# A two-layer transformer trunk on one core: the seven non-final experts of the first round written as straight code on TensorE, VectorE, ScalarE and SyncE

## What is computed

```python
def moe_swiglu(h, w_router, w_gu, w_down):
    t = h.reshape(-1, D)                                # 256 x 1024
    logits = (t @ w_router).astype(jnp.float32)
    top_val, top_idx = lax.top_k(logits, TOP_K)         # 2 of 8
    top_w = jax.nn.softmax(top_val, axis=-1)
    gates = jnp.sum(jax.nn.one_hot(top_idx, N_EXPERTS) * top_w[..., None], axis=1)
    out = jnp.zeros_like(t)
    for e in range(N_EXPERTS):
        out = out + gates[:, e:e + 1] * swiglu(t, w_gu[e], w_down[e])
    return out.reshape(B, S, D)
```

## Time and profile before

| | us |
|---|---|
| median of 3 runs | 1356.4 (1354.75 to 1358.1) |
| the profiled execution's own time | 1348.95 |
| its span, first to last instruction | 1347.1 |
| its mean granted TensorE clock | 0.979 of full |

### The profile page before, as it was taken

One profiled execution on the slowest core, in us unless ns is written; L12 is line 12 of the kernel. 1 busy time (PEld: TensorE's weight loads), 2 busy tenths in 40 slices (PEclk: granted clock), 3 DMA queues, 4 the chain that ended last, 5 costly groups with the idle time before them and its releaser, 6 DMA issues.

```text
span 1347.1 us, 41800 instructions
## 1 busy us (share of the span) xinstructions
PE 1289.3 (96%) x18773; PEld 859.4 (64%) x18773; DVE 416.9 (31%) x658; ACT 237.0 (18%) x377; POOL 78.1 (6%) x101
## 2 busy tenths in 40 slices
PE   6999999999999999999899899989989998999996
PEld 4499999899776666665566455545645564566653
DVE  6867778788851001101010110010110011002003
ACT  3254443465730001001000000000000000000001
POOL 2610000000120000000000000000000000000001
PEclk9999999999989999999899899989989998999998
DMA  9998999779199999999999999989999999999980
GB/s 360 409 344 296 331 320 338 280 273 383 50 388 408 408 390 397 408 402 404 343 409 398 344 392 398 409 300 406 398 343 388 398 410 326 393 395 396 410 323 34
DMA packets 210338, 478.39 MB, mean 355 GB/s; under 512 B 15072, under 2 KB 38704, under 8 KB 210032
## 3 DMA queue, kind: packets, MB, share of 16 engines
q1 hardware_dynamic: 204928, 457.76, 89.2%
q0 software_dynamic: 5088, 17.59, 4.3%
q10 hardware_dynamic: 144, 0.26, 0.1%
HBM read 465.98 MB, written 11.15 MB: 354 GB/s over the span
## 4 chain that ended last, share of the span: by engine, by line
PE 94%; issue 3%; DVE 1%; ACT 1%; DMA 1%; POOL 0%; SPq 0%; DVEq 0%; POOLq 0%
PE ps L2152 44%; PE ps L2159 22%; PE ps L1698 7%; PE ps L1700 7%; PE ps L1699 7%; PE ps L1789 1%; DMA raw<-w_mod 1%; PE ps L1778 1%; PE ps L1682 1%; PE ps L1986 0%; PE ps L2117 0%; PE ps L1716 0%; PE ps L2075 0%; PE ps L2108 0%; PE ps L1756 0%
## 5 line engine op out<-in xcount | busy, mean ns | idle before, releaser
L2152 PE MATMUL ps<-raw,turned_in 128*32 128x256 f32 x4704 | 276.6, 389 | 28.0 <-issue 28.0
L2152 PE MATMUL ps<-ring_w,turned_in 128*32 128x256 f32 x4560 | 259.3, 379 | 0.0
L2152 PEld LDWEIGHTS ps<-raw,turned_in 128*32 128x32 f32 x4704 | 154.8, 112 | 143.4 <-issue 45.0
L1572 DVE TENSOR_TENSOR tmp<-tmp,ps 128x384 f32<-128x384 f32 x56 | 31.0, 554 | 691.5 <-ACT tmp L1052 691.5
L2152 PEld LDWEIGHTS ps<-ring_w,turned_in 128*32 128x32 f32 x4560 | 147.6, 110 | 101.6
L1052 ACT ACTIVATE tmp<-ps 128x384 f32<-128x384 f32 x56 | 27.4, 490 | 838.9 <-PE ps L2152 838.9
L1698 PE MATMUL ps<-thi,whi 128*128 128x256 f32 x480 | 135.9, 283 | 2.1 <-DVE tlo L1126 2.1
L2159 PE MATMUL ps<-ring_w,turned_act 128*32 128x256 f32 x2352 | 137.6, 380 | 0.0
L1699 PE MATMUL ps<-tlo,whi 128*128 128x256 f32 x480 | 135.8, 283 | 0.0
L1700 PE MATMUL ps<-thi,wlo 128*128 128x256 f32 x480 | 135.8, 283 | 0.0
L2159 PE MATMUL ps<-raw,turned_act 128*32 128x256 f32 x2208 | 125.4, 379 | 0.0
(11 more groups left out here) (281 smaller groups left out, 1014.3 us busy)
## 6 DMA issues: line engine op xcount, KB each, us to landing
raw<-moe_w_gu SPq DMA_DIRECT2D x196, 512.0 KB, 7.0
ring_w<-moe_w_gu SPq DMA_DIRECT2D x190, 512.0 KB, 7.3
ring_w<-moe_w_down SPq DMA_DIRECT2D x98, 512.0 KB, 7.3
raw<-moe_w_down SPq DMA_DIRECT2D x92, 512.0 KB, 7.5
raw<-w_mod SPq DMA_DIRECT2D x88, 512.0 KB, 6.0
rows<-moe_w_gu SPq DMA_DIRECT2D x62, 512.0 KB, 7.7
raw<-ffn_w_gu SPq DMA_DIRECT2D x44, 512.0 KB, 5.5
rows<-moe_w_down SPq DMA_DIRECT2D x34, 512.0 KB, 6.5
```

What stands on the lines that cost most here:

```text
L1572: dve.tensor_tensor(actf_e.rearrange("p (g j) -> p g j", g=GROUPS), sg_e.rearrange("p (g j) -> p g j", g=GROUPS), gate_up_ps(c, 1), ALU.mu ...
L2152: mm = pe.matmul(tile_out(j, 2 * (c % 2) + g // 2, (g % 2) * 256, 256), g_t[:, k, 32 * g:32 * g + 32], w[:, kk, :, :, 32 * j:32 * j + 32], ...
```

## The change

In the first round (`ps_no == 0`) the hardware loops over experts become Python loops, so that each pass is written out, with the expert's number a constant. In the later rounds, behind the `If`, the hardware loops stay. GpSimd is not touched. Nothing in a pass is removed, added or reordered but what handled the expert's number and the loop.

```diff
@@ sync, experts
                 gate_up(0, 0, 0, 0, False, False)
-                with sp.Fori(0, NE - 1) as e:
-                    expert(e, False)
+                if ps_no == 0:
+                    for e in range(0, NE - 1):
+                        expert(e, False)
+                else:
+                    with sp.Fori(0, NE - 1) as e:
+                        expert(e, False)
@@ scalar, experts
                 expert(0, True, False)
-                with act.Fori(1, NE - 1) as e:
-                    expert(e, False, False)
+                if ps_no == 0:
+                    for e in range(1, NE - 1):
+                        expert(e, False, False)
+                else:
+                    with act.Fori(1, NE - 1) as e:
+                        expert(e, False, False)
@@ vector, experts
-                with dve.Fori(1, NE - 1) as e:
-                    expert(e, False, False)
+                if ps_no == 0:
+                    for e in range(1, NE - 1):
+                        expert(e, False, False)
+                else:
+                    with dve.Fori(1, NE - 1) as e:
+                        expert(e, False, False)
@@ tensor, experts
-                with pe.Fori(1, NE - 1) as e:
-                    expert(e, False, False)
+                if ps_no == 0:
+                    for e in range(1, NE - 1):
+                        expert(e, False, False)
+                else:
+                    with pe.Fori(1, NE - 1) as e:
+                        expert(e, False, False)
```

## The result

| | before | after |
|---|---|---|
| median, us | 1355.58 (4 runs, 1354.49 to 1358.1) | 1310.01 (4 runs, 1307.77 to 1311.79) |
| the profiled execution, us | 1348.95 | 1308.8 |
| its span, us | 1347.1 | 1307.0 |
| its mean granted TensorE clock | 0.979 | 0.992 |

The ratio is 0.966, with a 95% interval of 0.9638 to 0.9683: 45.6 us less on the medians, 40.15 us less on the profiled executions. 1312 us had been forecast.

A forecast was written before the change was run, and what follows sets the result against it. TensorE, busy 96% of the span, was taken to bound the kernel. Removing its five branches back saves 43.8 us, all else 0: 1356.4 - 43.8 = 1312.6, rounded to 1312 us, range 1303 to 1324.

The forecast's parts named there:

- the sum's 1305.2: Profiled execution of 1348.95 us less 43.8 us; the 7.45 us from profile to median was then kept, giving 1312 us.
- The five branches, 43.8 us: TensorE's five branches back between experts: standing and slow matmuls go, saving 43.8 us; bounds 28.0 to 43.8 us.
- The bound from below, 28.0 us of standing: Least saving on TensorE's five branches, 28.0 us, if the slow matmuls stayed slow for another reason.
- The clock: TensorE's granted clock falls to 0.50 after a stand; without stands at expert borders it was to stay at 1.00.
- the row: Profile's 4.72 us before the first matmul after a TensorE branch, chosen over the skill page's price of about 108 ns.
- The other engines at nothing: VectorE's, ScalarE's and SyncE's removed branches, and GpSimd unchanged: 0 us, as they lay in waiting or spare time.
- The transfers at nothing: Weight transfers lose 2.3 us an expert, 18 us over eight, against 27 us in hand: 9 left, so 0 us.
- The check against SP's last issue of before: SP issued its last unit at 1295.70, 0.05 us after TensorE freed its slot; taken as support for transfers costing 0 us.
- more than the sum: Rival: the 7.45 us between profile and median lie in the branches and go too, 1305 us; chance 0.12.
- The transfers take part of it back: Rival: shortfall above 3.4 us an expert makes TensorE wait for landings in experts 5 to 7, 1321 us; chance 0.12.
- The branch is not it: Rival: the 4.7 us belongs to the expert border, or something equal replaces it; no change, 1356 us; chance 0.03.
- starving for instructions: Rival: TensorE's straight code arrives late by DMA, 1.91 us for each of 80 packets, 1465 us; chance 0.03.

The follow-up runs named there:

- The experiment with a bare stand: Changed kernel with TensorE also waiting for VectorE's last output ahead of experts 2 to 6, no branch there: 1337.14 us.
- the hinted runs: Kernel before, TensorE's branch back hinted so its target is fetched ahead: 1339.14 us; with its loop head also at a block's start: 1314.34 us.
- the loop with head and hint: Kernel before with TensorE's loop head at the first slot of a 256-instruction block and its branch back hinted: 1314.34 us.
- the run with fewer bytes: Changed kernel loading 3.1% fewer bytes an expert from expert 1 on, with the same TensorE work: 1307.83 us.
- the runs with TensorE's head moved or hinted: Kernel before with TensorE's loop head at a block's start, 1344.08 us; with its branch back hinted, 1339.14 us; with both, 1314.34 us.

## Why the prediction was right, and where it was not

*The forecast, 1312 us, and the 1310.01 us measured.* The agreement is in part luck. The profiled execution came out 3.6 us above the sum's 1305.2, and the median 1.2 us above the profiled execution, where 7.45 us had been kept. The two misses are of opposite sign, and 2.6 us are left of them.

*The five branches, 43.8 us.* Right in place and size. Every pass is 110.30 us, as was taken from the first pass. In the profiled executions the experts got 41.73 us shorter, which is 43.77 less the 2.04 us of the transfers. The bound from below, 28.0 us of standing, left out the slow matmuls, and these did go with the stands.

*The clock.* Right: 1.00 in every pass. The experiment with a bare stand shows that a stand is enough to bring it down.

*The price of a branch in the Trainium skill (Advanced Engine Details and Errata, Control Flow Timing), 108 ns.* The choice to go by the row was right, and the runs say what the two prices are. With the code at hand, as in the hinted runs, the chain shows no gap at the branch, and a pass of the loop with head and hint takes 110.30 us, as a straight one does. So nothing of the size of the 4.7 us is left without the fetch.

*The other engines at nothing.* Right, shown by the three kernels with one or three engines in loops.

*The transfers at nothing.* This is the step that failed, by a small amount. "9 us are left" was worked out from a shortfall of 0.91 MB in one pass. The seamless passes show 0.83, 1.31, 1.30, 1.52, 1.27 and 1.39 MB for experts 1 to 6, 7.6 MB or some 20 us of transfers at the queue's own 387 GB/s (42.73 MB in 110.30 us). The pass I had taken, expert 1, was the mildest of them. The landing that TensorE waited for at 1212.30 is that of unit 306, counted along the chain. Its slot was free at 1177.9, the transfer was issued at 1196.7 and took 15.0 us to land. So it was 18.8 us late in being issued and 8 us slower than the 6.8 of the earlier trace rows, together the 27 us of lead. The missing bytes give 20 us of these. The other 7 stay open: they may be units that are partly moved while they count as not landed, which no run tested. The check against SP's last issue of before, on time at 1295.70, misled: less than two experts had gone by since the last stall. In the same way the rate was to be 400 GB/s throughout, and it is 395 to 397 from expert 2 on. The cost was 2.0 us, inside the bounds of 0 to 18.

*What was not in the sum.* The profiled execution came out 3.6 us above 1305.2. 2.0 are the transfers, 1.6 are from before the experts, which begin at 407.69 instead of 406.05. In 33 to 66 us the granted clock is 0.90 where it was 0.95. It is not the change's: the run with fewer bytes, straight on all four engines, has 0.95 there, and the runs with TensorE's head moved or hinted have 0.90. Over all the profiles the experts begin anywhere from 405.67 to 410.33 us.

*The 7.45 us between profile and median.* In the changed kernel this distance is 1.2 us, so the medians fell by more than the sum, 45.6 us. That leans to the rival "more than the sum", in which the branches cost more in the other runs than in the one profiled. The record has two things for it. The five branches cost 43.8 us in the profile of before, and 46.4 us in that of TensorE alone in its loop, the same code on TensorE (28.0 and 29.4 us of standing). And the 37 runs of the kernel before that stood beside the experiments go from 1346.10 us at a granted clock of 0.985 to 1360.83 us at 0.974, slower as the clock is lower. But the profile of before also had one of the earliest starts of the experts, 406.05 us, and that has nothing to do with the branches. How the 7.45 us divide is not shown: the unprofiled runs have no trace.

*The rivals.* The transfers take part of it back: true as a mechanism, at 2 us instead of 9. Its sign, waits for landings in experts 5 to 7, came, and at a shortfall of some 3.3 us a pass, just below the 3.4 that had been set as the condition. The branch is not it, and starving for instructions: both excluded. Over 884 us TensorE stood for no instruction of the straight code, behind DMA engines at a share of 1.04.

## What to carry to other kernels

Here, a gap of a few us on the bounding engine that waited for no semaphore, and came at every pass but the first, was the fetch of the loop's code. If you see one like it, compare the first pass with the second, and you have its price before you change anything. Only that engine needed straight code, or a loop whose head starts a block and whose branch is hinted, which gave all but 4 to 5 us of it here. Then ask what the gaps were good for: count what the transfers lose in each seamless pass, over several passes and not one, because the stalls you remove were also the time in which they caught up.

## What the runs showed of the hardware

- A branch back on TensorE to a loop of some 4000 instructions costs 4.6 to 5.2 us of standing, then matmuls at half clock, and often a second stand of 0.2 to 2.4 us. The whole is 7.8 to 12.0 us with the head where it was, and 6.3 to 7.7 us with the head at the start of a block, where no second stand came.
- With the hint alone 25 matmuls follow the branch without a gap, and then TensorE stands for 3.3 to 3.5 us. Head and hint together leave no stand; at the exit a hinted loop stands for 4.0 to 5.1 us where the plain one has no gap.
- A stand of 3.65 us without a branch brings the granted clock from 1.00 down to 0.64 on average over the next 4.7 us, at a cost of 1.9 us in slower matmuls.
- One core sustained 395 to 397 GB/s in all for 550 us, with its 16 DMA engines at a share of 1.04 throughout.
